# The last two groups of a gated FFN accumulate their w_down products together; the last output leaves in smaller pieces

## The chip, the cores and the metric

One Trainium2 chip, eight cores, each running the same program on its own eighth of the sequence. No core exchanges anything with another. The time is the device time of the slowest core, in microseconds (us).

## The reference, cut to what matters

```python
h = h + (gate_a * y_conv + gate_b * y_mla) @ w_o      # 2048 channels, token mixers before it
u = rmsnorm(h, ln2_g)
a = causal_dwconv3(u @ w_ffn_up, ffn_conv_w) + ffn_conv_b   # 2 x 5632 channels
a_gate, a_up = jnp.split(a, 2, axis=-1)
h = h + (jax.nn.silu(a_gate) * a_up) @ w_ffn_down     # 5632 -> 2048, this sum is the output
```

The product with `w_ffn_down` (in the kernel `w_dn`) sums over 5632 channels. A sum over channels may be cut into parts and added up in any order.

## The kernel before, in words

Each core has 1024 of its own positions, held as 8 blocks of 130 (128 and a halo of 2), and keeps everything with channels on the 128 partitions. After the mixers, the residual stream lies in SBUF as `hres`, 16 tiles of 128 channels in float32, and its scaled copy for the FFN as `u2`, 16 tiles in bf16.

The FFN runs over 44 blocks of 128 channels in four groups of 11. `up(j)` makes one block: 96 matmuls (gate and up halves, three column pieces of 390, 390 and 260, 16 input tiles), six VectorE operations that scale it out of PSUM by the norm, then the convolution with three taps on VectorE, Silu on ScalarE, and one product that writes the block as `fT[g % 2][:, jj, :]` in bf16. There are two such buffers, for the group being made and the one before it.

`down(g)` multiplies the 11 blocks of group g with `w_dn`: for each of the 16 output tiles c and each half t of 512 positions, 11 matmuls accumulate in one PSUM bank. Outputs are taken in pairs, so four banks are filled in a row. For groups 0 to 2 VectorE adds each bank to `hres` in place. For group 3 it adds bank and `hres` into a staging tile `ost`, and SyncE's queue writes 256 KB from there to `outT`. `down(0)`, `down(1)` and `down(2)` stand right behind the first `up` of the following group, `down(3)` behind the last `up`; it is the last stage of the program.

The staging tile has two slots, one for each output of a pair, and each slot is one object for the recorder that derives the waits (`Tost[x]`), though it holds both halves:

```python
    ost, Tost = Pool_(A6, ARENA).slabs(2, [OWN], F32, "ost")
...
                    tt(dst, PS[ps[x][t]].rearrange("p (b n) -> p b n", n=128), hh, ALU.add,
                       [TP[ps[x][t]], Th[c]], [Th[c]] if g < 3 else [Tost[x]])
```

So the addition for the second half of an output waits until the transfer of the first half, which reads the same object, has landed.

What sets the order: each engine runs its own list in the order of the calls; `S.add` records each call with what it reads and writes, and `finalize` turns that into waits on semaphores. `bank(8)` hands out the eight PSUM banks in turn. The weights of the FFN come through a ring of four slots ("A"): `weight_plan` lists the blocks in order of use, `wget` and `wdone` mark a block as taken and as done, and GpSimd issues the load of the next block in the plan as soon as the matmuls that read its slot are done. The list of the plan also sets where a block lies in `wall`, so a changed plan moves bytes in HBM, not their number. `out00` to `out11` are the channels (semaphores) of the output transfers.

Of the kernel before, what the change touches and what calls it, by code (L numbers as in the profile page):

```python
# [6 lines left out]
F32 = mybir.dt.float32  # L7
# [4 lines left out]
ALU = mybir.AluOpType  # L12

PE, ACT, DVE, POOL, SP = "tensor", "scalar", "vector", "gpsimd", "sync"
# [328 lines left out]
BW = 130  # L343
# [10 lines left out]
OWN = 1024  # L354
QSCALE = 192.0 ** -0.5
KB = 1024
ARENA = 208896
# [16 lines left out]
def weight_plan():  # L374
    plan = []
    for i in range(6):
        plan.append((("qlat", i), "w_in", 0, 16, 3072 + 128 * i, 128))
    for i in range(8):
        plan.append((("zv", i), "w_in", 0, 16, 2048 + 128 * i, 128))
        plan.append((("zc", i), "w_in", 0, 16, 1024 + 128 * i, 128))  # L380
        plan.append((("zb", i), "w_in", 0, 16, 128 * i, 128))
    for c in range(16):
        plan.append((("ga", c), "w_in", 0, 16, 4416 + 128 * c, 128))
        plan.append((("gb", c), "w_in", 0, 16, 6464 + 128 * c, 128))
        plan.append((("co", c), "w_co", 0, 8, 128 * c, 128))
        plan.append((("mo", c), "w_mo", 0, 16, 128 * c, 128))
    for c in range(16):
        plan.append((("wo", c), "w_o", 0, 16, 128 * c, 128))

    def up(j):  # L390
        plan.append((("fg", j), "w_up", 0, 16, 128 * j, 128))
        plan.append((("fu", j), "w_up", 0, 16, DFF + 128 * j, 128))

    def down(g):
        for c in range(16):
            plan.append((("fd", g, c), "w_dn", g * 1408, 11, 128 * c, 128))

    for g in range(4):
        for jj in range(11):
            up(g * 11 + jj)  # L400
            if g > 0 and jj == 0:
                down(g - 1)
    down(3)
    for h in range(NH):
        if h % 2 == 0:
            plan.append((("hq", h // 2), "wq", 0, 6, 192 * h, 384))
        plan.append((("hkv", h), "w_kvb", 0, 4, 256 * h, 256))
    return plan
# [11 lines left out]
def build_program():  # L420
    nc = bass.Bass("TRN2", target_bir_lowering=False)  # L421

    def din(name, shape, dt=F32):
        return nc.dram_tensor(name, list(shape), dt, kind="ExternalInput").ap()

    plan = weight_plan()
    woffs, wtotal = plan_offsets(plan)
    xg = din("xg", [NKB * 128, 16 * 128])
# [6 lines left out]
    outT = nc.dram_tensor("outT", [D, OWN], F32, kind="ExternalOutput").ap()  # L435
# [6 lines left out]
    PS = [psum[:, 512 * i:512 * i + 512] for i in range(8)]  # L442
    TP = [T("ps%d" % i, excl=True) for i in range(8)]
    S = Sched(nc)

    def esz(dt):
        return 2 if dt == BF16 else 4

    def V(off, shape, dt):
        nb = int(np.prod(shape)) * esz(dt)  # L450
        assert off % 4 == 0 and off + nb <= ARENA, (off, nb)
        v = arena[:, off:off + nb].bitcast(dt)
        if len(shape) == 2:
            v = v.rearrange("p (a b) -> p a b", b=shape[1])
        return v
# [47 lines left out]
    def width(ap):  # L503
        n = 1
        for d in ap.shape[1:]:
            n *= d
        return n

    def mm(out, lhsT, rhs, start, stop, reads, writes):
        S.add(PE, lambda e: e.matmul(out, lhsT=lhsT, rhs=rhs, start=start, stop=stop), reads, writes,  # L510
              cost=max(width(rhs) / 2400.0, 0.055) + 0.003)
# [7 lines left out]
    def dcost(out, *ins):  # L519
        fast = all(x.dtype == BF16 for x in (out,) + ins)  # L520
        return width(out) / (1920.0 if fast else 960.0) + 0.069
# [5 lines left out]
    def tt(out, in0, in1, op, reads, writes, held=0.0):  # L527
        S.add(DVE, lambda e: e.tensor_tensor(out=out, in0=in0, in1=in1, op=op), reads, writes,  # L528
              cost=dcost(out, in0, in1) + held)
# [13 lines left out]
    def dma(eng, out, in_, chan, reads=(), writes=()):  # L543
        S.add(eng, lambda e: e.dma_start(out=out, in_=in_), reads=reads, writes=writes, chan=chan,  # L544
              cost=in_.shape[0] * width(in_) * esz(in_.dtype) / 2.7e5)
# [44 lines left out]
    def wpump():  # L590
        for name in wslots:
            ns = len(wslots[name])
            while wloc[name] < min(len(wqueue[name]), wlimit.get(name, 1 << 30)):
                s = wloc[name] % ns
                if not wfree[name][s]:
                    break
                b = wqueue[name][wloc[name]]
                _, _, _, k, _, n = plan[b]
                dst = V(wslots[name][s], [k * n], BF16)
                src = wall[woffs[b]:woffs[b] + 128 * k * n].rearrange("(p f) -> p f", p=128)  # L600
                dma(POOL, dst, src, "w%s%d" % (name, s), writes=[wT[name][s]])
                wfree[name][s] = False
                whome[b] = (name, s)
                wloc[name] += 1

    def wget(key):
        b = windex[key]
        wpump()
        assert b in whome, key
        name, s = whome[b]  # L610
        _, _, _, k, _, n = plan[b]
        return V(wslots[name][s], [k, n], BF16), wT[name][s]

    def wdone(key):
        name, s = whome[windex[key]]
        wfree[name][s] = True
        wpump()
# [42 lines left out]
    for i in range(3):  # L660
        v, t = P1.tile([16, 128], F32, "xw%d" % i)
# [367 lines left out]
    def bank(n=5):  # L1029
        b = bk[0] % n  # L1030
        bk[0] += 1
        return b
# [54 lines left out]
    for n in range(18):  # L1087
        if n == 4:
            st_l.units.append(Unit(krot, 0.0, pos=-9.0))
        i, t = divmod(n, 3)  # L1090
        st_l.units.append(Unit(lambda i=i, t=t: ql(i, t), 2.6, need=Tu, pos=-9.0, bank=True))
        if n > 0:
            i, t = divmod(n - 1, 3)
# [8 lines left out]
    for i in range(2):  # L1102
        v, t = P4.slabs(8, [512], BF16, "Kn%d" % i)
# [4 lines left out]
    for i in range(2):  # L1108
        v, t = P4.tile([NA], BF16, "Qn%d" % i)
        Qn.append(v)  # L1110
        TQn.append(t)
        v, t = P4.tile([NA], BF16, "Qr%d" % i)
# [17 lines left out]
    for i in range(2):  # L1130
        v, t = P4.slabs(8, [512], BF16, "Vh%d" % i)
# [328 lines left out]
    c, n = 0.0, 0  # L1460
# [89 lines left out]
    for c in range(16):  # L1550
        for key, dst, Td, bo in (("ga", sga, Tsga, 0), ("gb", sgb, Tsgb, 16)):
            w, Tw = wget((key, c))
            for t, (off, n) in enumerate(T3):
                p = bank(8)
# [6 lines left out]
        for t, (off, n) in enumerate(T3):  # L1561
            x = t % 2
# [14 lines left out]
    hres, Th = PB.slabs(16, [NA], F32, "h")  # L1577
    PC = Pool_(Tm[15].hi, ARENA)
    u2, Tu2 = PC.slabs(16, [NA], BF16, "u2")
    sq2, Tsq2 = PC.slabs(3, [390], BF16, "sq2")  # L1580
    rstd2, Trstd2 = PC.slabs(3, [390], F32, "rstd2")
    A6 = PC.p
# [8 lines left out]
    for c in range(16):  # L1591
        w, Tw = wget(("wo", c))
        for t, (off, n) in enumerate(T3):
            p = bank()
# [20 lines left out]
    fT, TfT = [], []  # L1615
    v, t = Pool_(A6, ARENA).slabs(11, [OWN], BF16, "fT0")
    fT.append(v)
    TfT.append(t)
    v, t = PF.slabs(11, [OWN], BF16, "fT1")
# [3 lines left out]
    def up(j):  # L1623
# [17 lines left out]
        act(yg[:, 0, :], yg[:, 0, :], AF.Silu, Tyg, Tyg)  # L1641
        tt(fT[gb][:, jj, :], yg[:, 0, :], yu[:, 0, :], ALU.mult, Tyg + Tyu, [TfT[gb][jj]])

    def down(g):
        gb = g % 2
        for c0 in range(0, 16, 2):
            ws = [wget(("fd", g, c)) for c in (c0, c0 + 1)]
            ps = [[bank(8), bank(8)] for _ in range(2)]

            for j0, j1 in ((0, 9), (9, 11)) if g == 3 and c0 == 0 else ((0, 11),):  # L1650
                for x in range(2):
                    for t in range(2):
                        for jj in range(j0, j1):
                            mm(PS[ps[x][t]], ws[x][0][:, jj, :], fT[gb][:, jj, 512 * t:512 * t + 512], jj == 0, jj == 10,
                               [ws[x][1], TfT[gb][jj]], [TP[ps[x][t]]])
            for x in range(2):
                c = c0 + x
                wdone(("fd", g, c))
                h3 = hres[:, c, :].rearrange("p (b n) -> p b n", n=BW)
                for t in range(2):  # L1660
                    hh = h3[:, 4 * t:4 * t + 4, 2:130]
                    dst = hh if g < 3 else ost[:, x, 512 * t:512 * t + 512].rearrange("p (b n) -> p b n", n=128)
                    tt(dst, PS[ps[x][t]].rearrange("p (b n) -> p b n", n=128), hh, ALU.add,
                       [TP[ps[x][t]], Th[c]], [Th[c]] if g < 3 else [Tost[x]])
                    if g == 3:
                        dma(SP, outT[c * 128:(c + 1) * 128, 512 * t:512 * t + 512], ost[:, x, 512 * t:512 * t + 512],
                            "out%d%d" % (x, t), reads=[Tost[x]])

    for g in range(4):
        for jj in range(11):  # L1670
            up(g * 11 + jj)
            if g > 0 and jj == 0:
                down(g - 1)
    ost, Tost = Pool_(A6, ARENA).slabs(2, [OWN], F32, "ost")
    down(3)
    S.emit(final_waits=["out00", "out01", "out10", "out11"])
    return nc


# [4 lines left out]
def prepare_inputs(x, positions, ln1_g, w_in, b_gate, conv_w, w_conv_out, q_a_g, w_q_b, kv_a_g, w_kv_b,  # L1684
# [14 lines left out]
            "w_mo": np.asarray(w_mla_out, f32)[0], "w_o": np.asarray(w_o, f32)[0],  # L1699
            "w_up": np.asarray(w_ffn_up, f32)[0], "w_dn": np.asarray(w_ffn_down, f32)[0]}  # L1700
    plan = weight_plan()
    offs, total = plan_offsets(plan)
    wall = np.empty((total,), f32)
# [89 lines left out]
```

How the kernel before makes its waits and increments, by code:

```python
        def replay(e, eng):  # L192
            sem_e = sched.eng_sem[e]
            for o in sched.ops[e]:
                for (sem, v) in o.waits:
                    eng.wait_ge(sem, v)
                ins = o.fn(eng)
                if o.is_dma:
                    ins.then_inc(sched.chan_sem[o.chan], 16)
                elif o.needs_inc:
                    ins.then_inc(sem_e, 1)
# [18 lines left out]
            @block.sync  # L220
            def _(eng):
                replay(SP, eng)
                for ch in final_waits:
                    eng.wait_ge(sched.chan_sem[ch], 16 * sched.chan_cnt[ch])
```

## Time and profile before

| | |
|---|---|
| time of the runs | median 2624.53 us of 3 (2618.39 to 2768.56) |
| profiled execution, its own time | 2624.36 us |
| its span, slowest core (core 1) | 2622.7 us |
| fastest core (core 7) | 2611.1 us |
| TensorE busy with matmuls | 2544.1 us, 97% of the span, 18338 matmuls |
| VectorE busy | 1506.5 us, 57% |
| ScalarE busy | 1036.7 us, 40% |
| moved by the core's 16 DMA engines | 195.69 MB, mean 75 GB/s |

All times of rows are those of core 1 where nothing else is said, counted from the start of its span; 1.66 us of the execution's own time lie outside the span. Busy shares are averages over stages with different limits, so the stage that the change touches has to be read by itself: which engine is busy there, and which wait ends last.

### The profile page before, as it was taken

To read this page: it belongs to the slowest core of one execution; us is meant where nothing else is said; L and a number is where in the kernel's file an instruction comes from. 1 tells how busy PE (TensorE), PEld (TensorE's weight loads), DVE (VectorE), ACT (ScalarE), POOL (GpSimd) and SP (SyncE) were. 2 spreads that over 40 slices of the span, in tenths; PEclk is the share of its full clock that TensorE was granted. 3 is DMA by queue.
4 is the path that set the end of the run, shared out by engine and by line. 5 is a ranking of instruction groups with operands and counts; after the bars stand their busy time and mean duration, and the time that the engine had idled before them with its cause. 6 is when DMAs were issued, how large, how long until landed. Compare 5 with 4: busy or idle time off the path is not lost.

```text
span 2622.7 us, 51998 instructions; the slowest of 8 cores (2611.1 to 2622.7 us)
## 1 busy us (share of the span) xinstructions
PE 2544.1 (97%) x18338; PEld 1636.1 (62%) x18338; DVE 1506.5 (57%) x3051; ACT 1036.7 (40%) x2044; POOL 184.1 (7%) x321
## 2 busy tenths in 40 slices
PE   4999999999999999999999999999999999999997
PEld 2886666666666666666666666666456646655653
DVE  3881787777877778751212212377447727754752
ACT  4883688888888788851111113300000000000000
POOL 1010000000000000000000000011110111010100
PEclk9999999999999999999999999999999999999999
DMA  8674011202020202344444465444454454445445
GB/s 189 167 146 74 15 28 32 42 19 44 13 51 14 47 10 47 88 93 72 74 77 74 73 148 135 73 73 71 72 84 75 69 83 77 75 68 86 75 85 149
DMA packets 64636, 195.69 MB, mean 75 GB/s; under 512 B 7232, under 2 KB 8512, under 8 KB 63296
## 3 DMA queue, kind: packets, MB, share of 16 engines
q0 software_dynamic: 45648, 144.33, 33.7%
q1 hardware_dynamic: 18736, 48.03, 5.7%
q8 instruction: 154, 2.52, 0.4%
q14 instruction: 98, 0.80, 0.1%
HBM read 320.30 MB, written 15.83 MB: 128 GB/s over the span
## 4 chain that ended last, share of the span: by engine, by line
PE 88%; DVE 4%; DMA 4%; issue 2%; ACT 1%; SPq 0%; DVEq 0%; ACTq 0%; POOL 0%; POOLq 0%
PE ps L510 88%; DMA outT<-arena 2%; DVE arena L528 2%; DVE arena L524 2%; DMA arena<-wkvin 1%; ACT arena L517 1%; DMA arena<-xg 0%; SPq L544 0%; DVEq L196 0%; DVE arena L541 0%; DVE arena L537 0%; DVE arena L534 0%; ACTq L196 0%; SPq L196 0%; POOL arena L544 0%
## 5 line engine op out<-in xcount | busy, mean ns | idle before, releaser
L510 PE MATMUL ps<-arena 128*128 128x390 bf16 (+9 forms) x18338 | 2544.1, 300 | 63.9 <-ACT arena L517 41.3
L510 PEld LDWEIGHTS ps<-arena 128*128 128x128 bf16 x18338 | 1636.1, 98 | 971.4 <-issue 120.4
L528 DVE TENSOR_TENSOR arena<-ps,arena 128x390 f32<-128x390 f32 (+6 forms) x744 | 374.8, 511 | 806.9 <-PE ps L510 719.4
L528 DVE TENSOR_TENSOR arena<-arena 128x130 bf16<-128x130 bf16 (+17 forms) x1522 | 664.5, 474 | 245.1 <-ACT arena L517 218.5
L517 ACT ACTIVATE arena<-ps,arena 128x260 bf16<-128x260 f32 (+7 forms) x992 | 517.8, 546 | 422.4 <-PE ps L510 374.2
L517 ACT ACTIVATE arena<-arena 128x256 f32<-128x256 f32 (+14 forms) x412 | 268.4, 676 | 913.0 <-DVE arena L524 790.6
L524 DVE SCALAR_TENSOR_TENSOR arena<-arena 128x1024 f32<-128x1024 f32 (+9 forms) x499 | 371.4, 761 | 38.2 <-ACT arena L517 13.4
L517 ACT ACTIVATE arena<-ps 128x512 bf16<-128x512 f32 (+11 forms) x635 | 317.3, 523 | 133.3 <-PE ps L510 130.0
L544 POOL DMA_DIRECT2D arena<-wall x286 | 167.1, 585 | 2259.6 <-PE ps L510 2199.1
L537 DVE TENSOR_SCALAR arena<-arena 128x1024 f32<-128x1024 f32 (+1 forms) x90 | 72.3, 803 | 0.0
L524 DVE SCALAR_TENSOR_TENSOR arena<-ps,arena 128x256 bf16<-128x256 f32 (+1 forms) x80 | 33.2, 465 | 12.1 <-PE ps L510 6.9
L544 POOL DMA_DIRECT2D arena<-xg x30 | 16.0, 550 | 144.8 <-PE ps L510 53.2
L534 DVE TENSOR_SCALAR arena<-arena 128x390 f32<-128x390 f32 (+2 forms) x29 | 16.3, 562 | 1.7 <-DVE arena L541 0.2
L517 ACT ACT_TABLE_LOAD x5 | 6.4, 1283 | 27.3 <-DVE arena L524 14.6
L528 DVE TENSOR_TENSOR arena<-arena,ps 128x390 bf16<-128x390 f32 (+1 forms) x24 | 12.2, 510 | 0.4 <-DVE arena L524 0.3
L541 DVE COPY arena<-ps 128x2 f32<-128x2 f32 (+1 forms) x32 | 7.1, 221 | 2.1 <-PE ps L510 1.7
L541 DVE CAST arena<-arena 128x1028 f32<-128x1028 int32 (+1 forms) x5 | 3.5, 697 | 5.1 <-DMA arena<-posg 4.7
L541 DVE COPY arena<-arena 128x6 f32<-128x6 f32 (+1 forms) x24 | 3.8, 159 | 0.8
L544 POOL DMA_DIRECT2D arena<-cst x1 | 1.0, 982 | 0.0
L768 DVE MEMSET arena<- 128x128 bf16 x1 | 0.2, 165 | 1.2 <-PEq L421 1.2
L961 DVE MEMSET arena<- 64x512 bf16 x1 | 0.5, 485 | 0.1
L421 POOL MEMSET const-float32-0.0<- 128x1 f32 x1 | 0.1, 98 | 0.5 <-issue 0.5
(3 smaller groups left out, 0.3 us busy)
## 6 DMA issues: line engine op xcount, KB each, us to landing
arena<-wall POOLq DMA_DIRECT2D x182, 512.0 KB, 5.4
arena<-wall POOLq DMA_DIRECT2D x64, 352.0 KB, 4.5
arena<-xg POOLq DMA_DIRECT2D x22, 512.0 KB, 9.6
arena<-xo SPq DMA_DIRECT2D x16, 520.0 KB, 22.9
arena<-xg SPq DMA_DIRECT2D x8, 1024.0 KB, 6.3
arena<-wall POOLq DMA_DIRECT2D x32, 256.0 KB, 3.7
outT<-arena SPq DMA_DIRECT2D x32, 256.0 KB, 3.4
arena<-wkvin SPq DMA_DIRECT2D x16, 320.0 KB, 16.3
```

Of the source, the lines that this page charges most:

```text
L421: nc = bass.Bass("TRN2", target_bir_lowering=False)
L510: S.add(PE, lambda e: e.matmul(out, lhsT=lhsT, rhs=rhs, start=start, stop=stop), reads, writes, cost=max(width(rhs) / 2400.0, 0.055) + 0.003)
L517: S.add(ACT, lambda e: e.activation(out=out, in_=in_, func=func, **kw), reads, writes, cost=c)
L524: S.add(DVE, lambda e: e.scalar_tensor_tensor(out=out, in0=in0, scalar=scalar, in1=in1, op0=op0, op1=op1), reads, writes, cost=dcost(out, ...
L528: S.add(DVE, lambda e: e.tensor_tensor(out=out, in0=in0, in1=in1, op=op), reads, writes, cost=dcost(out, in0, in1) + held)
L534: S.add(DVE, lambda e: e.tensor_scalar(out=out, in0=in0, scalar1=s1, scalar2=None, op0=op0), reads, writes, cost=c)
L537: S.add(DVE, lambda e: e.tensor_scalar(out=out, in0=in0, scalar1=s1, scalar2=s2, op0=op0, op1=op1), reads, writes, cost=c)
L541: S.add(DVE, lambda e: e.tensor_copy(out=out, in_=in_), reads, writes, cost=dcost(out, in_))
L544: S.add(eng, lambda e: e.dma_start(out=out, in_=in_), reads=reads, writes=writes, chan=chan, cost=in_.shape[0] * width(in_) * esz(in_.dtyp ...
L768: S.add(DVE, lambda e: e.memset(ones, 1.0), writes=[Tones], cost=0.2)
L961: f_t.units.append(Unit(lambda: S.add(DVE, lambda e: e.memset(sqkr[64:128, :, :], 0.0), writes=Tsqkr), 0.0, pos=-8.5))
```

## The change

`down(2)` is no longer called. `fT[0]` keeps group 2 until the end, and after the last `up` one stage makes the products of groups 2 and 3 for each output into the same bank: 22 matmuls in a row, one addition with `hres` (which by then holds groups 0 and 1), one transfer. For the first two outputs all products of group 2 come first (four banks), then those of group 3. The staging tile lies where `u2` was and has four slots of 512 positions, each an object and a channel of its own; output c and half t use slot 2 (c mod 2) + t. The last half of the last output is made in two pieces of 256 positions, both in slot 3. The weight plan follows: the blocks of group 2 move from the start of group 3 to the end, each beside its block of group 3.

```diff
@@ weight_plan
-            if g > 0 and jj == 0:
+            if g in (1, 2) and jj == 0:
                 down(g - 1)
-    down(3)
+    for c in range(0, 16, 2):
+        for g, x in ((2, 0), (2, 1), (3, 0), (3, 1)) if c == 0 else ((2, 0), (3, 0), (2, 1), (3, 1)):
+            plan.append((("fd", g, c + x), "w_dn", g * 1408, 11, 128 * (c + x), 128))
@@ build_program
+    def products(g, c, p, o, n, start, stop):
+        w, Tw = wget(("fd", g, c))
+        for jj in range(11):
+            mm(PS[p][:, 0:n], w[:, jj, :], fT[g % 2][:, jj, o:o + n], start and jj == 0, stop and jj == 10,
+               [Tw, TfT[g % 2][jj]], [TP[p]])
...
+    def out(c, p, o, n):
+
+        hh = hres[:, c, :].rearrange("p (b n) -> p b n", n=BW)[:, o // 128:(o + n) // 128, 2:130]
+        x = 2 * (c % 2) + o // 512
+        d = ost[:, x, o % 512:o % 512 + n]
+        tt(d.rearrange("p (b n) -> p b n", n=128), PS[p][:, 0:n].rearrange("p (b n) -> p b n", n=128), hh, ALU.add,
+           [TP[p], Th[c]], [Tost[x]])
+        dma(SP, outT[c * 128:(c + 1) * 128, o:o + n], d, "out%d" % x, reads=[Tost[x]])
...
-    ost, Tost = Pool_(A6, ARENA).slabs(2, [OWN], F32, "ost")
-    down(3)
-    S.emit(final_waits=["out00", "out01", "out10", "out11"])
+    ost, Tost = Pool_(Tu2[0].lo, Tu2[15].hi).slabs(4, [512], F32, "ost")
+
+    ps = [[bank(8), bank(8)] for _ in range(2)]
+    for g in (2, 3):
+        for c in range(2):
+            for t in range(2):
+                products(g, c, ps[c][t], 512 * t, 512, g == 2, g == 3)
+                if g == 3:
+                    out(c, ps[c][t], 512 * t, 512)
+            wdone(("fd", g, c))
+    for c in range(2, 16):
+        for o, n in ((0, 512), (512, 512)) if c < 15 else ((0, 512), (512, 256), (768, 256)):
+            p = bank(8)
+            for g in (2, 3):
+                products(g, c, p, o, n, g == 2, g == 3)
+            out(c, p, o, n)
+        for g in (2, 3):
+            wdone(("fd", g, c))
+    S.emit(final_waits=["out%d" % x for x in range(4)])
```

`down(g)` for groups 0 and 1 takes one output at a time instead of a pair; its matmuls stand in the same order. Line numbers behind the plan move by 2.

Three places in the order of the instructions. The first is GpSimd's list of weight loads from the end of `down(1)` on; a row is a line of the code, the operation, destination and source, the size per partition and how many stand in a row (128x2048 is a block for `up`, 128x1408 one for `down`). Before:

```order
L544 DMA arena<-wall 128x2048 x22
L544 DMA arena<-wall 128x1408 x16
L544 DMA arena<-wall 128x2048 x22
L544 DMA arena<-wall 128x1408 x16
L544 DMA arena<-wall 128x2048 x20
L544 DMA arena<-wall 128x1408 x16
L203 UNCONDITIONAL_BRANCH
```

Now:

```order
L546 DMA arena<-wall 128x2048 x22
L546 DMA arena<-wall 128x1408 x16
L546 DMA arena<-wall 128x2048 x42
L546 DMA arena<-wall 128x1408 x32
L203 UNCONDITIONAL_BRANCH
```

The 16 blocks of group 2 have moved behind the 20 last blocks of `up`, next to the 16 of group 3; on TensorE the 352 matmuls of `down(2)` have moved the same way.

The second is TensorE at the start of the last stage, with the semaphores that an instruction waits for (`dsem_wA2` is a weight slot's load, `sem_vector` is VectorE). Before:

```order
L510 MATMUL ps<-arena 128x512 [waits dsem_wA2,sem_vector]
L510 MATMUL ps<-arena 128x512 x8
L510 MATMUL ps<-arena 128x512 [waits sem_vector]
L510 MATMUL ps<-arena 128x512 x8
L510 MATMUL ps<-arena 128x512 [waits dsem_wA3,sem_vector]
L510 MATMUL ps<-arena 128x512 x8
L510 MATMUL ps<-arena 128x512 [waits sem_vector]
L510 MATMUL ps<-arena 128x512 x9
L510 MATMUL ps<-arena 128x512 [waits sem_vector]
L510 MATMUL ps<-arena 128x512 x6
```

Now:

```order
L512 MATMUL ps<-arena 128x512 [waits dsem_wA2,sem_vector]
L512 MATMUL ps<-arena 128x512 x10
L512 MATMUL ps<-arena 128x512 [waits sem_vector]
L512 MATMUL ps<-arena 128x512 x10
L512 MATMUL ps<-arena 128x512 [waits dsem_wA3,sem_vector]
L512 MATMUL ps<-arena 128x512 x10
L512 MATMUL ps<-arena 128x512 [waits sem_vector]
L512 MATMUL ps<-arena 128x512 x10
L512 MATMUL ps<-arena 128x512 [waits dsem_wA0]
L512 MATMUL ps<-arena 128x512 x9
L512 MATMUL ps<-arena 128x512 [waits sem_vector]
L512 MATMUL ps<-arena 128x512 x11
```

Before, the wait for the last blocks of `fT` (the last `sem_vector` of the piece) stands behind 36 matmuls. Now 54 stand ahead of it, 44 of group 2 and 10 of group 3.

The third is the end of VectorE's list, the last additions into the staging tile (`dsem_out` and a number is a channel of an output transfer). Before:

```order
L528 TENSOR_TENSOR arena<-ps,arena 128x512 [waits sem_tensor,dsem_out01]
L528 TENSOR_TENSOR arena<-ps,arena 128x512 [waits sem_tensor,sem_vector,dsem_out00]
L528 TENSOR_TENSOR arena<-ps,arena 128x512 [waits sem_tensor,dsem_out11]
L528 TENSOR_TENSOR arena<-ps,arena 128x512 [waits sem_tensor,sem_vector,dsem_out10]
L203 UNCONDITIONAL_BRANCH
```

Now:

```order
L530 TENSOR_TENSOR arena<-ps,arena 128x512 [waits sem_tensor,sem_vector,dsem_out0]
L530 TENSOR_TENSOR arena<-ps,arena 128x512 [waits sem_tensor,sem_vector,dsem_out1]
L530 TENSOR_TENSOR arena<-ps,arena 128x512 [waits sem_tensor,sem_vector,dsem_out2]
L530 TENSOR_TENSOR arena<-ps,arena 128x256 [waits sem_tensor,sem_vector,dsem_out3] x2
L203 UNCONDITIONAL_BRANCH
```

Before, the second half of an output (`dsem_out00`, `dsem_out10`) waits for the transfer issued right after the addition ahead of it. Now each addition waits for the transfer issued four additions earlier, except the last of the two pieces of 256, which waits for that of the other piece.

## Rows read from the trace of the kernel before

**Rows 1.** The page: span, and part 4, the chain that ended last.

```profile
span 2622.7 us, 51998 instructions; the slowest of 8 cores (2611.1 to 2622.7 us)
...
PE ps L510 88%; DMA outT<-arena 2%; DVE arena L528 2%; DVE arena L524 2%; DMA arena<-wkvin 1%; ACT arena L517 1%; DMA arena<-xg 0%; SPq L544 0%; DVEq L196 0%; DVE arena L541 0%; DVE arena L537 0%; DVE arena L534 0%; ACTq L196 0%; SPq L196 0%; POOL arena L544 0%
```

**Rows 2.** Waits from 2527 us on: us in total, times, longest.

```profile
DVE arena L528 <- DMA outT<-arena: 62.6, 16, 8.3
...
PE ps L510 <- DVE arena L528: 3.6, 4, 1.5
```

**Rows 3.** The chain that ended last, 2480 us to end: start, us, what.

```profile
2479.84 47.64 PE ps L510 x325
...
2527.64 0.43 DVE arena L528
...
2535.17 1.24 DVE arena L528
...
2542.91 8.09 DMA outT<-arena
...
2605.78 2.13 DMA outT<-arena
...
2609.45 2.10 DMA outT<-arena
...
2617.39 2.12 DMA outT<-arena
2619.51 0.03 issue
...
2619.61 0.69 DVE arena L528
```

**Rows 4.** Timeline of the last stage, TensorE: start, us, what [idle before, releaser].

```profile
2536.55 32.53 PE L510 MATMUL ps<-arena 128*128 128x512 bf16 x150 [1.10 <-DVE arena L528]
...
2570.57 4.91 PE L510 MATMUL ps<-arena 128*128 128x512 bf16 x22 [1.48 <-DVE arena L528]
...
2575.72 14.65 PE L510 MATMUL ps<-arena 128*128 128x512 bf16 x66 [0.25 <-DVE arena L528]
...
2591.19 16.78 PE L510 MATMUL ps<-arena 128*128 128x512 bf16 x77 [0.82 <-DVE arena L528]
```

**Rows 5.** Timelines around `down(2)`: TensorE from 2240 us, two of GpSimd's loads.

```profile
2239.79 120.53 PE L510 MATMUL ps<-arena 128*128 128x390 bf16 x710
...
2315.53 0.53 POOL L544 DMA_DIRECT2D arena<-wall  x1 [3.84 <-PE ps L510]
...
2386.76 0.53 POOL L544 DMA_DIRECT2D arena<-wall  x1 [4.22 <-PE ps L510]
```

**Rows 6.** Timeline of VectorE in one `up` of group 3.

```profile
2511.74 0.56 DVE L528 TENSOR_TENSOR arena<-ps,arena 128x390 f32<-128x390 f32 x1 [1.45 <-PE ps L510]
2513.51 0.43 DVE L528 TENSOR_TENSOR arena<-ps,arena 128x260 f32<-128x260 f32 x1 [1.21 <-PE ps L510]
...
2525.86 0.56 DVE L528 TENSOR_TENSOR arena<-ps,arena 128x390 f32<-128x390 f32 x1 [1.44 <-PE ps L510]
```

**Rows 7.** Issue to landing: `wall` from 2394 us, `outT` from 2527, from 2590.

```profile
DMA to landing us min/median/max: 4.2/5.2/9.1
...
DMA to landing us min/median/max: 2.0/3.4/8.1
...
DMA to landing us min/median/max: 2.0/2.1/4.3
```

**Rows 8.** 256-wide work: TensorE's timeline near 110 us; VectorE's groups by shape.

```profile
110.33 29.90 PE L510 MATMUL ps<-arena 128*128 128x256 bf16 x277 [0.94 <-DVE arena L541]
...
L528 DVE TENSOR_TENSOR arena<-ps,arena 128x512 f32<-128x512 f32 x128 | 86.8, 690 | 201.0 <-PE ps L510 137.9 <-DMA outT<-arena 62.6
...
L528 DVE TENSOR_TENSOR arena<-ps,arena 128x256 f32<-128x256 f32 x16 | 6.7, 421 | 17.8 <-PE ps L510 17.6
```

**Rows 9.** Core 4: TensorE's last piece, and its waits from 2527 us.

```profile
2593.09 12.03 PE L510 MATMUL ps<-arena 128*128 128x512 bf16 x53 [1.35 <-DVE arena L528]
...
PE ps L510 <- DVE arena L528: 2.4, 2, 1.4
```

More of the change, by code:

```diff
@@ L1642, in up @@
         tt(fT[gb][:, jj, :], yg[:, 0, :], yu[:, 0, :], ALU.mult, Tyg + Tyu, [TfT[gb][jj]])
-    def down(g):
[L1645 to L1667, printed above, removed]
@@ new lines, in products @@
+    def products(g, c, p, o, n, start, stop):
[3 more added lines that the diff above has]
+               [Tw, TfT[g % 2][jj]], [TP[p]])
+    def down(g):
+        for c in range(16):
+            h3 = hres[:, c, :].rearrange("p (b n) -> p b n", n=BW)
+            ps = [bank(8), bank(8)]
+            for t in range(2):
+                products(g, c, ps[t], 512 * t, 512, True, True)
+            wdone(("fd", g, c))
+            for t in range(2):
+                hh = h3[:, 4 * t:4 * t + 4, 2:130]
+                tt(hh, PS[ps[t]].rearrange("p (b n) -> p b n", n=128), hh, ALU.add, [TP[ps[t]], Th[c]], [Th[c]])
@@ L1671, in build_program @@
             up(g * 11 + jj)
-            if g > 0 and jj == 0:
+            if g in (1, 2) and jj == 0:
                 down(g - 1)
-    ost, Tost = Pool_(A6, ARENA).slabs(2, [OWN], F32, "ost")
-    down(3)
-    S.emit(final_waits=["out00", "out01", "out10", "out11"])
+    ost, Tost = Pool_(Tu2[0].lo, Tu2[15].hi).slabs(4, [512], F32, "ost")
+    ps = [[bank(8), bank(8)] for _ in range(2)]
+    for g in (2, 3):
+        for c in range(2):
+            for t in range(2):
+                products(g, c, ps[c][t], 512 * t, 512, g == 2, g == 3)
[9 more added lines that the diff above has]
+        for g in (2, 3):
+            wdone(("fd", g, c))
+    S.emit(final_waits=["out%d" % x for x in range(4)])
     return nc
```

## The prediction

> **What bounds the kernel now.** I read the chain that ended last first, since it says which resource a shorter stage would have to relieve. TensorE holds 88% of it, but the second entry is the output transfer with 2%, some 52 us, and it can only come from the end of the program [rows 1]. The waits from 2527 us on confirm it: VectorE waited 62.6 us for landings of `outT`, 16 times, that is once for each output tile, and TensorE in turn 3.6 us for VectorE [rows 2]. The chain in order of time shows the form. It leaves TensorE when the last `up` ends (2479.84 + 47.64 = 2527.5), goes through the convolution of the last block to 2536.4, and from then to the end it runs through landings of `outT` and additions on VectorE, with landings between 2.1 and 8.1 us in these rows [rows 3]. This is the shared slot: for each output, one landing must pass before the second half may be added. Between two such landings at the quiet end lie 2609.45 - 2605.78 - 2.13 = 1.5 us of additions and issue, so an output costs 2.1 + 1.5 = 3.6 us at best, less than TensorE's time for it, but with a landing over about 3.2 us it costs more, and while weights are loaded the landings are longer [rows 3, 7]. VectorE falls behind, eight banks fill up, and TensorE stalls.
>
> The timeline of TensorE shows the result: pauses of 1.10, 1.48, 0.25 and 0.82 us, together 3.65, and a last matmul that ends at 2591.19 + 16.78 = 2607.97 [rows 4]. The span ends at 2622.7 [rows 1]. So 14.7 us at the end belong to the backlog of additions and transfers alone.
>
> Around `down(2)` nothing waits: TensorE runs from 2239.79 for 120.53 us without a pause, across the end of group 2, `up(33)` and most of `down(2)` [rows 5].
>
> **The change part by part.**
>
> *Moving the products of group 2.* The loads of its blocks follow TensorE, and between the two shown lie 15 blocks: (2386.76 - 2315.53) / 15 = 4.75 us for a block of 22 matmuls, 0.216 us each [rows 5]. `down(2)` is 16 x 4.75 = 76.0 us of pure TensorE time. Taken out there, all that follows comes 76.0 us earlier if the next `up` does not suffer. It should not: VectorE in an `up` has idle pieces of 1.45 and 1.21 us that end with TensorE (so it waits for matmuls, not the other way), and repeats every 2525.86 - 2511.74 = 14.12 us, TensorE's own time for an `up` [rows 6]. The last `up` then ends at 2527.5 - 76.0 = 2451.5. Together the two groups need 32 x 4.75 = 152.0 us. By itself the move gains nothing. The 32 additions into `hres` that go away, 32 x 0.69 = 22 us of VectorE [rows 8], were hidden behind TensorE: nothing either.
>
> *The wait for the last block of `fT`.* It is ready 2536.41 - 2527.5 = 8.9 us after the last `up` [rows 3]. Before, 36 x 0.216 = 7.8 us of matmuls stood ahead of it and 1.10 us was lost [rows 4]. Now 54 x 0.216 = 11.7 us stand ahead. The wait goes, with 2.8 us to spare.
>
> *The staging slots.* From the third output on, an addition comes every 4.75 us and its slot was last used four additions ago, 19 us; for the first slots of the third output it is 3 x 2.4 + 4.75 = 11.9 us. The longest landing was 8.1 us [rows 7]. So no addition waits for a landing, and the other three pauses go, 2.55 us. Each pause also left a slow restart: a piece of 22 matmuls alone took 4.91 us [rows 4], 0.16 over the 4.75, five pieces, 0.8 us. The last matmul thus ends at E = 2451.5 + 152.0 = 2603.5, which is 2607.97 less 3.65 and 0.8, the same from the other side. The bounds: the floor is 152.0, since nothing here runs matmuls of this shape faster; if every block took 4.91, 5.1 us more.
>
> *The last output in pieces.* 44 matmuls of 256 columns replace 22 of 512. A stretch mostly of that width had 277 in 29.90 us, 0.108 each [rows 8], half of 0.216: no cost. The gain is less than it looks. Both small pieces use slot 3. The second of three pieces ends at E - 22 x 0.108 = E - 2.4; its addition starts 0.16 later (2527.64 against 2527.48 [rows 3]), takes 0.42 [rows 8], the transfer is issued 0.1 later and lands 2.1 after that [rows 3], which is E + 0.4. Only then, 0.1 later (2619.51 to 2619.61 [rows 3]), can the third piece be added: 0.42, to E + 0.94. From the end of the last addition to the end of the span it is 2622.7 - (2619.61 + 0.69) = 2.4 us [rows 1, 3]. End: E + 3.3. With a slot of its own it would be 0.16 + 0.42 + 2.4 = E + 3.0, and with one undivided half E + 0.16 + 0.69 + 2.4 = E + 3.25. So the pieces are worth nothing as written. If the landing took 4.3 us, the longest near the end [rows 7], the end would be E + 5.5. I take 2.1, since nothing else is then moving: the last weight block is issued over 20 us earlier.
>
> The landing of 256 KB took 2.1 us with nothing beside it [rows 3]. The Trainium skill, "DMA: Bandwidth & Descriptors", section "Anatomy of one DMA — SWDGE (gpsimd) path", gives 2.0 us fixed and the bytes at 436 GB/s, mostly a wait for the write's receipt. By it a piece of 128 KB would land in an estimated 2.3 us, and half the bytes would save only 0.3 of 2.6; it speaks against smaller pieces as such, and the sum by it would end 0.2 to 0.4 us later.
>
> *Sum.* 2603.5 + 3.3 = 2606.8 for core 1, against 2622.7: 15.9 us, of which 4.5 in front of the last matmul and 11.4 behind it. Would another core now be the last? Core 4 waited less: its last matmul ended at 2593.09 + 12.03 = 2605.1 with 2.4 us of waits [rows 9], so it ends near 2602.4 + 3.3 = 2605.7, still before core 1. With the 1.66 us outside the span, 2608.5 us. The profiled execution, 2624.36, is as long as the median, 2624.53, so this stands for the median too: 0.6% faster.
>
> **The rivals.** *The last piece lands late.* The slot shared by the last two pieces is named in the order of VectorE's list, so this wait is certain; open is its length. At 4.3 us for a landing the end is E + 5.5, that is 2609.0, or 2610.7 with what lies outside. Together with restarts that stay (up to 5.1), 2615.8. For it: the landings at the end were between 2.0 and 4.3 [rows 7]. Against it: the median there is 2.1, and now the pieces come 2.4 us apart, where before two additions in a row each sent their transfer.
>
> *Weights come late, and the kernel becomes slower.* An output now needs two blocks in 9.5 us as before, but of the four slots two are held at once by the output in work: the slot of group 2 is free only after three quarters of it, 7.1 us, that of group 3 at its end. The blocks that follow in these slots are needed 19.0 us after the start of this output, and 2.4 us later: 11.9 us for each. Loads landed in 4.2 to 9.1 us [rows 7], so they hide. From 11.9 us on, each further us is paid once in two outputs, seven times over the last 14; to lose the gain of 15.9 us it takes 2.3 us more, a landing of 14.2 us throughout, and at 16 us the time would be 2608.5 + 7 x 4.1 = 2637. For it: both weights and outputs use the same 16 engines. Against it: the output traffic per us is half of that in the old last stage, where 9.1 was the longest.
>
> *The gain goes elsewhere.* If pauses in the last stage are not caused by the slots but by the additions themselves, they stay (3.65 us), and only the backlog behind the last matmul shrinks: 2606.8 + 4.5 + 1.7 = 2613. Against it: VectorE's waits name the landings 16 times, and an addition is 0.69 us in 2.4.
>
> **How the numbers follow.** The forecast, all slot waits gone and the weights hidden, has 0.80. A late last piece or surviving pauses, 2610 to 2616, have 0.13 together. Weights late to the point of slower than before, 0.03; a gain beyond 20 us 0.04, for which I see only that single runs lie as low as 2618.39. For the range I take 6 us of spread between the runs shown below 2624.53, so down to 2601, and up to the second group's end: 2616. More than 2% (52 us) in either direction, about what a measurement of this kernel can tell from no change, is outside the forecast: faster by that would need TensorE's work to shrink, 0.01; slower needs landings of some 22 us, 0.02; within 2%, 0.97.
>
> **What would show it.** In the changed trace: no TensorE pause between the last `up` and the end, about 154 us long; VectorE's waits for `outT` reduced from 16 to one, of some 0.4 us or less beyond the matmuls; the last matmul within 3.5 us of the end; `up(33)` and `up(34)` back to back with the period of 14.12. I am wrong if TensorE waits for `wall` in that stage, if a block of 22 takes longer than 4.75 us there, if VectorE's `up` falls behind once `down(2)` is gone, or if the end of another core comes later than core 1's.

## The result

The changed kernel takes 2607.99 us in the median of 4 runs (2606.94 to 2608.76). Its ratio to the kernel before is 0.9938, 95% interval [0.9912, 0.9965]: 0.6% less time, clear of zero and within 2%. Ratios here and below leave out runs in which the cores of a die were disturbed, for either kernel. The profiled execution took 2606.94 us, 17.4 less than that of before.

The page of the changed kernel, its span and the second line of part 4 (shares of the chain that ended last, by line), answers to [rows 1]:

```profile
span 2605.4 us, 51950 instructions; the slowest of 8 cores (2597.8 to 2605.4 us)
...
PE ps L512 93%; ACT arena L519 1%; DMA arena<-wkvin 1%; DVE arena L530 1%; DVE arena L526 1%; DMA arena<-xg 0%; SPq L546 0%; DVE arena L543 0%; DVEq L196 0%; DVE arena L536 0%; ACTq L196 0%; POOL arena L546 0%; POOLq L196 0%; SPq L196 0%
```

The transfers of `outT`, second in that line before, are no longer in it, and TensorE's share has gone from 88 to 93%. The slowest core is now core 5; its rows follow. The waits from 2446 us on answer to [rows 2]:

```profile
DVE arena L530 <- PE ps L512: 122.1, 34, 4.4
...
DVE arena L530 <- DMA outT<-arena: 2.0, 1, 2.0
```

VectorE now waits for TensorE; of the 16 waits for a landing one is left. TensorE waits for nothing, which its timeline from 2200 us on shows in one row (answers to [rows 4, 5]), and the windows of the last stage confirm:

```profile
2199.79 402.77 PE L512 MATMUL ps<-arena 128*128 128x390 bf16 x2432
```

```profile
2450.57:2602.56 151.99, 151.99 (x726) 70.82 (x724) 30.17 (x40) 1.06 (x1) 15.73 (x29) 1.00 0.64 124
```

The columns of the second are the stretch, its length, busy us of TensorE, weight loads, VectorE, ScalarE and GpSimd (with counts), granted clock, share of the DMA engines, GB/s. All 726 matmuls of the last stage run in 151.99 us without a pause.

The timeline of VectorE at the end answers to the end of [rows 3]:

```profile
2593.25 0.69 DVE L530 TENSOR_TENSOR arena<-ps,arena 128x512 f32<-128x512 f32 x1 [4.06 <-PE ps L512]
2598.35 0.69 DVE L530 TENSOR_TENSOR arena<-ps,arena 128x512 f32<-128x512 f32 x1 [4.41 <-PE ps L512]
2600.40 0.42 DVE L530 TENSOR_TENSOR arena<-ps,arena 128x256 f32<-128x256 f32 x1 [1.36 <-PE ps L512]
2602.80 0.42 DVE L530 TENSOR_TENSOR arena<-ps,arena 128x256 f32<-128x256 f32 x1 [1.98 <-DMA outT<-arena]
```

TensorE's last matmul ends at 2199.79 + 402.77 = 2602.56 and the span at 2605.4: 2.84 us lie behind it, where 14.7 did. (Spans are printed to 0.1 us; the records behind them give 2.81.)

### The profile page after: what moved, and what is told of

Same layout as the page of the kernel before. It is cut to its first block, busy times and chain, and to the rows that moved or that the text cites. A ratio compares the mean times of both kernels' runs of the same rounds, so it can differ in the third digit from the quotient of the medians.

```text
span 2605.4 us, 51950 instructions; the slowest of 8 cores (2597.8 to 2605.4 us)
## 1 busy us (share of the span) xinstructions
PE 2545.5 (98%) x18360; PEld 1639.3 (63%) x18360; DVE 1486.7 (57%) x3020; ACT 1036.3 (40%) x2044; POOL 184.3 (7%) x321
## 4 chain that ended last, share of the span: by engine, by line
PE 93%; DVE 2%; DMA 2%; issue 1%; ACT 1%; SPq 0%; DVEq 0%; ACTq 0%; POOL 0%; POOLq 0%
PE ps L512 93%; ACT arena L519 1%; DMA arena<-wkvin 1%; DVE arena L530 1%; DVE arena L526 1%; DMA arena<-xg 0%; SPq L546 0%; DVE arena L543 0%; DVEq L196 0%; DVE arena L536 0%; ACTq L196 0%; POOL arena L546 0%; POOLq L196 0%; SPq L196 0%
## 5 line engine op out<-in xcount | busy, mean ns | idle before, releaser
L530 DVE TENSOR_TENSOR arena<-ps,arena 128x390 f32<-128x390 f32 (+6 forms) x713 | 354.2, 502 | 812.3 <-PE ps L512 784.9
```

## The experiments

### Four slots alone

```diff
-    ost, Tost = Pool_(A6, ARENA).slabs(2, [OWN], F32, "ost")
+    ost, Tost = Pool_(A6, ARENA).slabs(4, [512], F32, "ost")
...
-                       [TP[ps[x][t]], Th[c]], [Th[c]] if g < 3 else [Tost[x]])
+                       [TP[ps[x][t]], Th[c]], [Th[c]] if g < 3 else [Tost[2 * x + t]])
```

(made in the kernel before; destination and transfer use the slot `2 * x + t` too)

> The kernel before with four staging slots of 512 positions and nothing else changed. Theory S (a second half that waits for the landing of the first half's transfer is what cost the time): an addition now waits for a transfer issued four additions, 9.5 us, earlier; the longest landing was 8.1, so the three pauses of TensorE with their restarts (2.55 + 0.65 us) and the backlog behind the last matmul (11.4 us) go, while the pause of 1.10 at the start stays: 14.6 us less, ratio 0.994, VectorE's waits for outT near zero, the last matmul 3.2 us before the end. Rival M (what counts is that groups 2 and 3 are accumulated together, so that outputs come half as often): ratio 1.000, 16 waits for outT as before.

Measured: ratio 0.9947 [0.9932, 0.9961]. The timeline of TensorE on the slowest core, core 2:

```profile
2429.81 110.94 PE L510 MATMUL ps<-arena 128*128 128x390 bf16 x737
2541.85 68.15 PE L510 MATMUL ps<-arena 128*128 128x512 bf16 x308 [1.10 <-DVE arena L528]
```

and the waits of VectorE for landings there:

```profile
DVE arena L528 <- DMA outT<-arena: 8.7, 5, 3.6
```

Only the pause of 1.10 us for the last block of `fT` stays, on every core, and the last matmul, at 2610.00, is 3.4 us ahead of the end of the span (2613.4). VectorE's waits were expected near zero; they were 5.3 to 16.4 us on the eight cores, with landings of up to 9.3 us on this one. TensorE waits for none of them. Theory S holds in what it says of TensorE and of the end, and rival M in its strict form (1.000) falls.

### Merging alone, with the old staging

```diff
-        d = ost[:, x, o % 512:o % 512 + n]
+        d = ost[:, c % 2, o:o + n]
...
-           [TP[p], Th[c]], [Tost[x]])
+           [TP[p], Th[c]], [Tost[c % 2]])
...
-    ost, Tost = Pool_(Tu2[0].lo, Tu2[15].hi).slabs(4, [512], F32, "ost")
+    ost, Tost = Pool_(Tu2[0].lo, Tu2[15].hi).slabs(2, [OWN], F32, "ost")
...
-        for o, n in ((0, 512), (512, 512)) if c < 15 else ((0, 512), (512, 256), (768, 256)):
+        for o, n in ((0, 512), (512, 512)):
```

> The changed kernel with the old staging: two slots, each one object for both halves, and the last output undivided. The strict form of theory S (the slots alone carry the gain, the merging none): 16 waits of VectorE of the old kind and a time near that of before, ratio 0.998 to 1.000. Its wide form (a backlog only grows if a landing and the additions take longer than TensorE for an output): an output now takes TensorE 9.5 us, a landing of 3 to 8 us and 1.5 us of additions fit, so VectorE may wait at times but TensorE never, and the end comes 3.25 us behind the last matmul: as the changed kernel, 15.9 us less than before, ratio 0.994. Rival M: the same 0.994. Together with the slots alone it tells the three apart.

Measured: ratio 0.9962 [0.9937, 0.9986], so faster than before. The waits of VectorE for landings and the timeline of TensorE on the slowest core, core 6:

```profile
DVE arena L530 <- DMA outT<-arena: 14.7, 4, 4.4
```

```profile
2429.77 177.72 PE L512 MATMUL ps<-arena 128*128 128x390 bf16 x880
```

TensorE has no pause on any core, and its last matmul (2607.49) is 3.3 us ahead of the end (2610.8). The strict form of theory S falls: the slots are not needed for the gain once the outputs come half as often. The wide form stands: an output now has 9.5 us of TensorE's time for a landing and its additions, and VectorE's waits no longer reach TensorE. The intervals of this kernel, of the slots alone and of the changed kernel overlap, so their times don't rank them; the table under "Why the prediction was right" does it by the traces.

### Moving without merging

```diff
-            if g > 0 and jj == 0:
+            if g in (1, 2) and jj == 0:
                 down(g - 1)
+    down(2)
```

(in the kernel before, in the plan and in the program)

> The kernel before with the products of group 2 moved to the end, ahead of those of group 3, but still added to the residual by themselves, and with the old shared slots. The sum says that moving alone gains only the wait for fT, 1.10 us and its restart of 0.16: 2623 where before is 2624.4, with the pauses and the 14.7 us behind the last matmul as before. A rival by which the interruption of the up blocks by the products cost something (a disturbed rhythm on VectorE or the weight ring) gives 5 us or more.

Measured: ratio 0.9989 [0.9962, 1.0016], no difference that shows. On the slowest core, core 7, the wait of 1.10 us is gone, the others are there (waits of TensorE and VectorE, then the last piece of TensorE's timeline):

```profile
PE ps L511 <- DVE arena L529: 4.9, 6, 1.8
```

```profile
DVE arena L529 <- DMA outT<-arena: 64.4, 16, 7.5
```

```profile
2603.05 7.28 PE L511 MATMUL ps<-arena 128*128 128x512 bf16 x33 [0.71 <-DVE arena L529]
```

16 waits for landings as before, and 2624.1 - 2610.33 = 13.8 us behind the last matmul. So the move alone doesn't bring the gain of the change. That it gains nothing but the small wait is not shown: the interval still holds the 5 us of the expectation's rival (0.998). Other cores look better than this one, too: on four of the eight TensorE has no pause at all in the last stage, and 7.9 to 14.4 us lie behind the last matmul, where before it was 11.7 to 15.5.

### Without the cover for the last block

```diff
-    for g in (2, 3):
-        for c in range(2):
...
-    for c in range(2, 16):
+    for c in range(16):
```

> The changed kernel, but the first two outputs are made like all others (both groups for one half, then for the next) and not with all of group 2 first. Only 11 + 10 matmuls, 4.5 us, then stand ahead of the first that needs the last block of fT, which is ready 8.9 us after the last up. If that step of the sum is right, TensorE pauses once for 4.4 us at the start of the last stage and the time is 4.4 us (up to 0.2 more for the restart) over the changed kernel, 2612.5. If the block were ready sooner, or the pause were made good later (for instance by weights that then lie ready), less than 2 us over it.

Measured: ratio to before 0.9956 [0.9937, 0.9974]; the interval overlaps that of the changed kernel, so the trace has to tell. The timeline of TensorE on the slowest core, core 0:

```profile
2429.82 23.74 PE L512 MATMUL ps<-arena 128*128 128x390 bf16 x152
2458.17 150.52 PE L512 MATMUL ps<-arena 128*128 128x512 bf16 x705 [4.61 <-DVE arena L530]
```

One pause of 4.61 us where 4.4 were expected, 4.60 or 4.61 on all eight cores, and nothing makes it good later. It costs more than its length. The last row above has 705 matmuls in 150.52 us. Two of 256 columns counted as one, they are 683 of 512, which at the 0.216 us of the changed kernel take 147.5. The windows of this core behind the pause show where the rest went (columns as in the result):

```profile
2458.17:2464.00 5.83, 5.83 (x14) 2.02 (x15) 0.69 (x1) 0.00 (x0) 0.01 (x1) 0.50 0.13 48
2464.00:2608.60 144.60, 144.60 (x692) 67.53 (x690) 21.16 (x31) 0.00 (x0) 14.76 (x28) 1.00 0.64 126
```

For 5.83 us the granted clock was 0.50, the 1.2 GHz level, and 14 matmuls took about twice their time; then it was 1.00 again. Ahead of the pause, and behind the pause of 1.10 us in the kernel before, it was 1.00. On the eight cores the last stage took 158.1 to 159.6 us instead of 151.99, so taking all of group 2 first is worth 6.1 to 7.7 us and not 4.4: the pause of 4.61 and 1.5 to 3.0 us at the lower clock.

### The last half of the last output

Undivided; pieces of 256 with a slot of its own for the last; pieces of 384 and 128, likewise; and pieces of 256 with a slot of its own, where SyncE's list ends with the waits for out1, out2, out3, out0 in this order.

```diff
-        x = 2 * (c % 2) + o // 512
+        x = 0 if o > 512 else 2 * (c % 2) + o // 512
...
-        for o, n in ((0, 512), (512, 512)) if c < 15 else ((0, 512), (512, 256), (768, 256)):
+        for o, n in ((0, 512), (512, 512)) if c < 15 else ((0, 512), (512, 384), (896, 128)):
```

(the edit of the third; the second has the line of `x` alone, the first `for o, n in ((0, 512), (512, 512)):`)

> The changed kernel with the last output's second half undivided (512 positions, slot 3). The sum of the prediction: the end comes 0.16 + 0.69 + 2.4 = 3.25 us behind the last matmul, where the changed kernel shows 2.84 (2602.56 to 2605.4). A rival by which the pieces matter (half the bytes land sooner and the addition is shorter) gives 3.7 us or more.

> The changed kernel with the last piece of 256 in slot 0, which is long free, and not in slot 3. The wait for the piece before it goes: VectorE waits for no landing of outT, the last addition starts right behind the last matmul (0.24 us behind it in the changed kernel), and the end comes 2.6 to 2.8 us behind the last matmul, against 2.84. If the shared slot cost nothing, 2.84.

> The changed kernel with the last half in pieces of 384 and 128 positions, the last one in slot 0. The last addition shrinks to about 0.3 us and its transfer to 64 KB: 2.4 to 2.7 us behind the last matmul. By the rival that a transfer has a fixed time whatever its size, 0.1 us less than with 256 and a slot of its own, by the addition alone. In the time of the whole, 0.1 to 0.4 us under the changed kernel, which cannot be told from it: ratio to before 0.994.

> The last piece of 256 in slot 0 again, and the waits at the end of SyncE's list in the order out1, out2, out3, out0, so that the channel of the last transfer is waited for last. With slot 0 and the order 0 to 3 the end came 3.0 us behind the last matmul, later than with the shared slot (2.84), though the last addition started equally soon (0.24 us). If the three waits that SyncE still passes after the one for the last transfer cost that 0.15 us, it is now 2.84 again. If the transfer itself lands later on that channel, 3.0.

The last additions of the undivided half, of 256 with its own slot, and of 128 with its own slot (timelines of VectorE on the slowest core of each):

```profile
2606.51 0.69 DVE L530 TENSOR_TENSOR arena<-ps,arena 128x512 f32<-128x512 f32 x1 [3.69 <-PE ps L512]
```

```profile
2602.35 0.42 DVE L530 TENSOR_TENSOR arena<-ps,arena 128x256 f32<-128x256 f32 x1 [1.98 <-PE ps L512]
```

```profile
2606.83 0.29 DVE L530 TENSOR_TENSOR arena<-ps,arena 128x128 f32<-128x128 f32 x1 [0.67 <-PE ps L512]
```

All but the third of these kernels ran once, so only traces are compared. The table takes times from the end of the last matmul, over the eight cores of each, in us:

| last piece | last addition starts | ends | its transfer, issue to landing | landing to end of span | end of span |
|---|---|---|---|---|---|
| 512 | 0.24 | 0.94 | 2.00 to 2.04 | 0.29 | 3.35 to 3.39 |
| 256, shared slot (the changed kernel) | 0.24 to 0.25 | 0.67 | 1.70 to 1.86 | 0.29 | 2.79 to 2.94 |
| 256, own slot | 0.24 | 0.67 | 1.72 to 1.84 | 0.45 | 2.96 to 3.08 |
| 128, own slot | 0.24 | 0.54 | 1.55 to 1.62 | 0.45 | 2.65 to 2.72 |
| 256, own slot, its channel waited for last | 0.24 to 0.25 | 0.67 | 1.73 to 2.09 | 0.29 | 2.81 to 3.18 |

The undivided half ends 0.1 us later than its sum of 3.25, so the pieces gain 0.5 us over it. A slot of its own gains nothing: the last addition starts 0.24 us behind the last matmul with either, and the 2.6 to 2.8 us expected of it were missed. The 0.15 us that it loses are those of the three waits that SyncE still passes after the one for the last transfer: from the landing to the end it is 0.45 us with them, and 0.29 again on every core once that channel is waited for last. Landings of up to 2.09 us hide this in the end of that run's spans. The smaller last piece pays the same 0.15 us. The kernel with 384 and 128 had a ratio to before of 0.9957 [0.9916, 0.9997], not to be told from the changed kernel; there is no version here that beats it measurably.

### Late weights, brought out by doubled loads

```diff
+                if twice and s >= 0:
+                    sp, Tsp = twice[0]
+                    dma(POOL, sp[:, s, :], src, "again%d" % s, writes=[Tsp[s]])
                 dma(POOL, dst, src, "w%s%d" % (name, s), writes=[wT[name][s]])
```

(`twice` is filled where the last stage begins; in the second kernel the condition is `s % 2 == 0`)

> The changed kernel with each of the last 28 blocks of w_dn loaded a second time into unused space (the result of that load is not read), to bring out the rival of late weights. The 16 DMA engines were busy for 0.64 of the last stage and loads take some 0.5 of that, so this asks for about 1.1 of them. By the price in the prediction, TensorE starts to wait for wall when a load lands later than about 11.9 us after its issue, 7 us for each further us: with landings of 14 us, 15 us more. By the share, the stage is bound by the transfers and lasts 1.1 to 1.17 of 152 us: 10 to 26 us more, less some 10 us that the four slots hold in advance. If the weights have more cover than the sum says, no waits for wall and the same time.

> The changed kernel with every second of the last 28 blocks of w_dn loaded a second time into unused space (not read). With all of them twice, landings had a median of 11.3 and a maximum of 16.4 us and TensorE waited 8 to 10 us on each core. With half, the transfers ask for about 0.85 of the DMA engines; if the cover of 11.9 us per block is right, landings of 6 to 10 us stay hidden: no waits for wall, spans as in the changed kernel. If TensorE waits for wall at landings below 11 us, the cover was worked out wrong.

With all loads twice, waits and landings (all loads, also those not read) on the slowest core, core 7:

```profile
PE ps L512 <- DMA arena<-wall: 8.3, 6, 2.3
```

```profile
DMA to landing us min/median/max: 4.2/11.3/16.4
```

With half of them, the windows of the last stage and the landings on the slowest core, core 4:

```profile
2450.00:2600.00 150.00, 150.00 (x708) 69.06 (x706) 30.77 (x42) 1.06 (x1) 23.20 (x43) 1.00 0.84 159
```

```profile
DMA to landing us min/median/max: 4.4/6.4/8.5
```

With half of them doubled, no core of the eight waits for weights: the blocks that are read landed within 8.5 us, at 0.82 to 0.86 of the DMA engines. With all, the engines are at 0.99 from 2450 to 2610 us on core 7, every core waits for `wall`, 8.0 to 10.4 us, and the last stage lasts 162.2 to 163.9 us, 10.2 to 12.0 more than in the changed kernel, the lower end of the 10 to 26 us that the share gave and less than the 15 by the price. (The span, 2618.9, is 13.5 more, of which 1.8 lie ahead of the stage.) The rest beyond the waits are restarts and, on cores 3 and 7, a lower clock: behind the longest pause of core 7, 2.33 us, the granted clock was 0.61 over the next 4.43 us.

Load by load, the cover of 11.9 us (from the issue of a load to the matmul that needs it) holds. Of the 240 loads of blocks that are read, on eight cores, 72 landed later than 11.9 us after their issue, and TensorE waited for 63 of them. 168 landed sooner, and it waited for 14 of them. Six of these took 11.6 to 11.9 us. The other eight, one on each core, took 9.8 to 11.0 us, and GpSimd issued them late, after 3.90 us without work where 1.3 us is usual at that place (the row of core 7):

```profile
2493.49 1.05 POOL L546 DMA_DIRECT2D arena<-wall  x2 [3.90 <-issue]
```

The price per us was not measured: the landings spread, and the prediction's formula, with the median of 11.3, would give none.

## Why the prediction was right

*What bounds the last stage.* Right: the waits for landings of the shared slot. Four slots alone remove all pauses but the first, and the backlog behind the last matmul. The prediction named only the slots as the reason; accumulating the two groups together is a second, sufficient one, because it doubles TensorE's time for an output from 4.75 to 9.5 us. The changed kernel does both, and the second of them finds no backlog left to remove. The stage by itself shows this without the spread that the cores bring from earlier stages: from the end of the last `up` (the start of its last addition less 0.16 us) to the end of the span, over the eight cores of each profiled execution, with 76.0 us for `down(2)` added where it lies elsewhere:

| kernel | mean, us | range |
|---|---|---|
| before | 170.7 | 164.9 to 176.0 |
| moved, not merged | 166.2 | 159.9 to 171.8 |
| changed, without the cover | 161.9 | 161.1 to 162.5 |
| slots alone | 156.6 | 156.6 to 156.8 |
| merged, old staging | 155.3 | 155.3 to 155.3 |
| changed | 154.8 | 154.8 to 154.9 |

The gain of 15.9 us that was summed for core 1 is the mean of the eight cores; on core 1 itself it was 16.5. What the slots alone leave over the changed kernel, 1.8 us, is the first pause with its restart and the undivided last half; what merging alone leaves, 0.5, is the undivided half.

*The move.* Right in that it costs nothing and is not the source of the gain; a few us of its own are neither shown nor excluded (170.7 and 166.2 above are one execution each). In the changed trace the additions of `up` repeat from 2279.47 to 2293.59, every 14.12 us, across the place where `down(2)` was:

```profile
2279.47 0.56 DVE L530 TENSOR_TENSOR arena<-ps,arena 128x390 f32<-128x390 f32 x1 [1.44 <-PE ps L512]
...
2293.59 0.56 DVE L530 TENSOR_TENSOR arena<-ps,arena 128x390 f32<-128x390 f32 x1 [1.44 <-PE ps L512]
...
2307.72 0.56 DVE L530 TENSOR_TENSOR arena<-ps,arena 128x390 f32<-128x390 f32 x1 [1.44 <-PE ps L512]
```

*The stage.* 152.0 us were summed, 151.99 measured, with the 44 matmuls of 256 columns at no cost. The restarts of 0.16 us went with the pauses.

*The wait for the last block.* Gone. Without its cover it is 4.61 us against 4.4 worked out, and 1.5 to 3.0 us at the lower clock come on top, for which the prediction's sum of pauses and restarts has no term.

*The end.* Summed E + 3.3, measured E + 2.84. Here a term was mis-sized, and a conclusion fell with it: "the pieces are worth nothing as written". The step used 2.1 us and 2.4 us, both of transfers of 256 KB, for pieces of 128 KB. From the end of an addition to the start of the one that waits for its landing it was 2.34 us for 256 KB before, and is 1.98 for 128 KB (the last row of the result's timeline):

```profile
2619.61 0.69 DVE L528 TENSOR_TENSOR arena<-ps,arena 128x512 f32<-128x512 f32 x1 [2.34 <-DMA outT<-arena]
```

From the last addition to the end of the span it is 2.18 instead of 2.40. The landing of the second piece therefore comes just as the third is ready, and the wait for slot 3 costs nothing. Two slips of the step change nothing: its terms for the third addition's end add up to E + 0.9 and not E + 0.94, and the last weight block is issued 18.5 us ahead of the last matmul (2584.05) and not over 20. The estimate from the Trainium skill ("DMA: Bandwidth & Descriptors", "Anatomy of one DMA — SWDGE (gpsimd) path") had the difference right, 0.3 us for 128 KB less, against 0.36 here; its fixed part of 2.0 us, given for transfers that GpSimd issues, is too high for these stores of SyncE's, whose shortest landings were 1.7 us in all.

*The slowest core.* Core 5 instead of core 1; the last matmuls of the eight cores now end between 2594.9 us (core 7) and 2602.6, a spread that stems from earlier stages. The sum for core 1 gave 2606.8, the slowest core shows 2605.4. That another core ends last was one of the prediction's own signs of being wrong. What it had wrong is that it carried core 1's lead over the others, and its start of the stage, from one execution to the next: core 1's last `up` ended at 2448.3 where 2451.5 was summed, and core 5, at 2450.6, came last. That the median of 2607.99 lies 0.5 us from the 2608.5 is therefore in part luck; what the sum got right is the stage with its end, 155.3 us against 154.8.

*The rivals.* Late weights did not occur (no wait for `wall`): the blocks landed within 8.3 us, under the cover of 11.9, and with doubled loads landings passed it only with the DMA engines at 0.99. A late last piece did not occur. Pauses of another origin did not remain.

## What to carry to other kernels

Compare, for each output, the compute time with the chain of addition, transfer and landing that one staging object forces; where the chain is longer, a backlog grows through the stage and is paid at its end, here with 14.7 us behind the last matmul. Either more objects (one for each transfer in flight) or more work per output cured it here, and one of the two was enough. Look also at what a pause of the bottleneck engine does behind it: one of 4.61 us here cost 6.1 to 7.7. For the very last output, size its pieces by landings of their own size, not by those of larger transfers.

## What the runs showed of the hardware

- A transfer of 128 KB to HBM released its waiter 0.36 us sooner than one of 256 KB (1.98 against 2.34 us from the end of the addition). The last transfers of all, with nothing beside them, landed 2.00 to 2.04 us after their issue for 256 KB, 1.70 to 1.86 for 128 KB and 1.55 to 1.62 for 64 KB, over the eight cores of one execution each.
- With all eight cores in the same stage, the granted clock of the last 152 us stayed at 1.00, the 2.4 GHz level, through a stretch of 402.77 us of matmuls without a pause; 512 columns with their own weights took 151.99 us / 704 = 0.216 us each throughout (two of 256 counted as one).
- Behind a pause of 4.61 us the granted clock was 0.50, the 1.2 GHz level, for 5.83 us on core 0 of the kernel without the cover, which cost it 3.0 us; behind pauses of 1.10 and 1.48 us of the kernel before it was 1.00.
- Each wait of SyncE for a semaphore that was long up took 0.05 us: three of them behind the last landing made the end 0.15 us later.
- With weight loads doubled, landings of `outT`, issued by SyncE, rose from a median of 3.0 to 8.6 us and those of `wall`, issued by GpSimd, from 5.0 to 11.3 us (loads that are not read included), with the DMA engines at a share of 0.99.
